# Four opening parts of the conditioning instead of two, six of their row blocks multiplied on TensorE in fp32

## What is computed

```
cond = jax.nn.silu(c) @ w_ada[l] + b_ada[l]
shift, scale, gate_raw = jnp.split(cond, 3, axis=-1)
h = x * (1.0 + scale[:, None]) + shift[:, None]
proj = h @ w_in[l]
```

## Time and profile before

| | us |
|---|---|
| median of 3 runs | 2113.29 (2106.57 to 2115.07) |
| profiled execution | 2106.91 |
| its span, first to last instruction | 2105.1 |
| PE busy in it | 1908.0 (91%) |
| DVE busy in it | 1003.5 (48%) |
| ACT busy in it | 855.7 (41%) |
| POOL busy in it | 695.8 (33%) |

### The profile page before, as it was taken

The page is one execution under the profiler, slowest core; times in us unless marked ns, Lnnn a source line. Parts: engine busy times, 40 slices in busy tenths (PEclk is TensorE's granted clock), DMA queues, the critical chain, the costliest instruction groups (busy, mean ns, idle before and its releaser), DMA issues.

```text
span 2105.1 us, 35718 instructions
## 1 busy us (share of the span) xinstructions
PE 1908.0 (91%) x14368; PEld 1523.4 (72%) x14368; DVE 1003.5 (48%) x1327; ACT 855.7 (41%) x1220; POOL 695.8 (33%) x486
## 2 busy tenths in 40 slices
PE   4999988899997999988799997989989999998977
PEld 3687877699774687877699774666756877776755
DVE  6566377633445118376632545668625213132232
ACT  2424465533523434465533524445534323333332
POOL 2454532300252335532300341333433543332312
PEclk9899999999998999999999999999999999999998
DMA  8662222200422322322200422312233221221211
GB/s 326 231 220 71 90 90 75 85 4 4 152 99 80 116 73 68 101 87 79 73 4 4 170 90 70 140 60 71 76 114 120 91 89 50 70 69 51 67 64 70
DMA packets 60827, 192.91 MB, mean 92 GB/s; under 512 B 5632, under 2 KB 5888, under 8 KB 60320
## 3 DMA queue, kind: packets, MB, share of 16 engines
q1 hardware_dynamic: 60704, 191.10, 26.4%
HBM read 173.25 MB, written 17.83 MB: 91 GB/s over the span
## 4 chain that ended last, share of the span: by engine, by line
issue 49%; PE 23%; POOL 18%; DVE 4%; ACT 4%; DMA 1%; POOLq 0%; DVEq 0%; ACTq 0%; SPq 0%
POOL w_lo_sb L716 17%; PE proj L1978 11%; PE aux L2187 3%; DVE area_sb L1288 2%; DMA w_raw_sb<-wall 1%; PE aux L2118 1%; PE aux L2244 1%; PE proj L2187 1%; PE aux L2241 1%; DVE area_sb L1552 1%; ACT L813 1%; ACT w_hi_sb L793 0%; DVE area_sb L1291 0%; ACT L921 0%; PE aux L2174 0%
## 5 line engine op out<-in xcount | busy, mean ns | idle before, releaser
L716 POOL TENSOR_TENSOR w_lo_sb<-w_raw_sb,w_hi_sb 128x512 fp32r<-128x512 f32 x462 | 677.6, 1487 | 1202.9 <-ACT w_hi_sb L793 1202.8
L1978 PE MATMUL proj<-act_hi_sb,w_hi_sb 128*128 128x512 f32 x1480 | 601.3, 406 | 28.3 <-POOL w_lo_sb L716 11.1
L1978 PE MATMUL proj<-act_hi_sb,w_lo_sb 128*128 128x512 f32 x1480 | 581.7, 393 | 0.0
L1978 PE MATMUL proj<-act_lo_sb,w_hi_sb 128*128 128x512 f32 x1480 | 581.6, 393 | 0.0
L793 ACT ACTIVATE w_hi_sb<-w_raw_sb 128x1024 fp32r<-128x1024 f32 x231 | 244.4, 1058 | 719.6 <-PE proj L1978 501.0
L1978 PEld LDWEIGHTS proj<-act_hi_sb,w_hi_sb 128*128 128x128 f32 x1480 | 281.6, 190 | 100.0 <-issue 33.0
L1978 PEld LDWEIGHTS proj<-act_lo_sb,w_hi_sb 128*128 128x128 f32 x1480 | 281.9, 190 | 62.0 <-issue 6.3
L1978 PEld LDWEIGHTS proj<-act_hi_sb,w_lo_sb 128*128 128x128 f32 x1480 | 281.1, 190 | 60.3
L1997 PE MATMUL aux<-act_hi_sb,w_hi_sb 128*128 128x512 f32 x336 | 138.0, 411 | 36.3 <-issue 23.4
L1288 DVE TENSOR_TENSOR area_sb<-area_sb 128x256 f32<-128x256 f32 (+2 forms) x208 | 140.6, 716 | 19.4 <-ACT area_sb L946 9.8
L1997 PE MATMUL aux<-act_lo_sb,w_hi_sb 128*128 128x512 f32 x336 | 135.2, 402 | 0.0
(11 more groups left out here) (251 smaller groups left out, 2558.7 us busy)
## 6 DMA issues: line engine op xcount, KB each, us to landing
w_raw_sb<-wall SPq DMA_DIRECT2D x231, 512.0 KB, 3.3
area_sb<-w_ada SPq DMA_DIRECT2D x32, 512.0 KB, 5.5
slots_sb<-w_ada SPq DMA_DIRECT2D x16, 512.0 KB, 8.3
gate_scr<-stage_sb SPq DMA_DIRECT2D x32, 256.0 KB, 2.2
area_sb<-gate_scr SPq DMA_DIRECT2D x8, 1024.0 KB, 9.1
x_scr<-area_sb SPq DMA_DIRECT2D x3, 2048.0 KB, 7.3
area_sb<-x_scr SPq DMA_DIRECT2D x3, 2048.0 KB, 10.2
area_sb<-lru_gates SPq DMA_DIRECT2D x1, 3584.0 KB, 13.1
```

The costliest lines, as they stand in the source:

```text
L716: nc.gpsimd.tensor_tensor(w_lo[:, b % 2, :, :].rearrange("p k n -> p (k n)")[:, half], w_raw[:, b % 2, half], w_hi[:, b % 2, :, :].rearran ...
L1978: ins = MM(bank, w[:, s, k, :], a[:, t, :], start=(start and i == 0), stop=(stop and i == len(terms) - 1))
```

## The change

Layer 0's conditioning comes in four parts q of 512 columns (shift and scale of channel tiles 2q and 2q+1) where it was two halves of 1024. w_ada's columns are rearranged for that outside the kernel. A load is 256 KB, and there are 32 of them, into twelve buffers in the same space. Part 0 has all eight row blocks on DVE; parts 1 to 3 have six (ADA_ROWS), and TensorE multiplies row blocks 6 and 7 from their load buffers by the column of c, in fp32, into the same PSUM column that takes the sum over DVE's accumulator. SP loads parts, x tiles and weight blocks 0 to 2 in turn. The derived columns follow all four parts on DVE.

```diff
+ADA_ROWS = (8, 6, 6, 6)
...
-            for half in range(2):
-                jobs.add(("ada", 0, half), 4 + half)
+            for q in range(4):
+                jobs.add(("ada", 0, q), 4 + q % 2)
...
-            def load_part(half, k):
-                n = KT * half + k
-                wait(sp, S("ada_used"), n - 5)
-                sp.dma_start(ada_part[:, n % 6], dram["w_ada"][0, k][:, D * half:D * half + D])\
-                    .then_inc(S(f"ada_part{n % 6}"), 16)
+            def load_part(q, k):
+                n = KT * q + k
+                if n > 11:
+                    old, row = (n - 12) // KT, (n - 12) % KT
+                    if row < ADA_ROWS[old]:
+                        sp.wait_ge(S("ada_used"), sum(ADA_ROWS[:old]) + row + 1)
+                    else:
+                        job_ready(sp, ("ada", 0, old))
+                sp.dma_start(ada_part[:, n % 12], dram["w_ada"][0, k][:, HALF * q:HALF * q + HALF])\
+                    .then_inc(S(f"ada_part{n % 12}"), 16)
...
-            for k in range(6):
-                load_part(0, k)
-            load_x(0)
-            load_x(1)
-            blocks_to(1)
-            load_part(0, 6)
-            load_part(0, 7)
-            load_x(2)
-            load_x(3)
-            blocks_to(2)
-            for k in range(KT):
-                load_part(1, k)
-            for m in range(4, KT):
-                load_x(m)
+            for q in range(4):
+                for k in range(KT):
+                    load_part(q, k)
+                load_x(2 * q)
+                load_x(2 * q + 1)
+                blocks_to(min(q + 1, 3))
...
-            conditioned(0, 0, ((0, 4), (8, 4)))
-            for m in range(5):
-                if m < 4:
+            for q in range(4):
+                for k in range(ADA_ROWS[q]):
+                    ada_part_step(q, k)
+                conditioned(0, q, ((2 * q, 2), (8 + 2 * q, 2)))
+                for m in (2 * q, 2 * q + 1):
                     modulated(0, m)
-                if m:
-                    low(SPLITS["h", 0] + m - 1, m - 1, ST[(m - 1) % 2])
-            for k in range(KT):
-                ada_part_step(1, k)
+                for m in (2 * q, 2 * q + 1):
+                    low(SPLITS["h", 0] + m, m, ST[m % 2])
...
-                def condition(half):
-
-                    pe.wait_ge(S("ada_used"), KT * (half + 1))
-                    x = job_open(pe, ("ada", 0, half))
-                    for j in range(8 * half, 8 * half + 8):
-
-                        at = 8 * (j % 8 // 4) + 4 * (j // 8) + j % 4
-                        ins = MM(x[:, at:at + 1], ada_acc[:, P * j:P * j + P], C("ones", 0, 1), start=True, stop=True)
-                    job_full(ins, ("ada", 0, half))
+                def condition(q):
+
+                    pe.wait_ge(S("ada_used"), sum(ADA_ROWS[:q + 1]))
+                    x = job_open(pe, ("ada", 0, q))
+                    rest = range(ADA_ROWS[q], KT)
+                    for k in rest:
+                        n = KT * q + k
+                        pe.wait_ge(S(f"ada_part{n % 12}"), 16 * (n // 12 + 1))
+                    for j in range(4):
+                        at = 8 * (j // 2) + 2 * q + j % 2
+                        ins = MM(x[:, at:at + 1], ada_acc[:, HALF * q + P * j:HALF * q + P * j + P], C("ones", 0, 1),
+                                 start=True, stop=not rest)
+                        for k in rest:
+                            ins = MM(x[:, at:at + 1], ada_part[:, (KT * q + k) % 12, P * j:P * j + P],
+                                     DV["c"][:, k:k + 1], start=False, stop=(k == KT - 1))
+                    job_full(ins, ("ada", 0, q))
...
-                             ready=lambda k: condition(1) if (l, k) == (0, 4) else None)
+                             ready=lambda k: condition(k // 2) if l == 0 and k in (2, 4, 6) else None)
```

More of the change, by code:

```diff
@@ L442, in build @@
         later_acc = area[:, 18:24].rearrange("p a t -> p (a t)")
[L443 removed]
+        ada_part = slots[:, 5:8].rearrange("p a b t -> p (a b) t")
         def wait(eng, semaphore, value):
@@ L1325, in ada_add, with ada_part_step @@
                 ins.then_inc(S("ada_used"), 1)
-            def ada_part_step(half, k):
-                n = KT * half + k
-                dve.wait_ge(S(f"ada_part{n % 6}"), 16 * (n // 6 + 1))
-                wait(dve, S("ada_used"), n)
-                ada_add(ada_acc[:, D * half:D * half + D], ada_part[:, n % 6], k)
+            def ada_part_step(q, k):
+                n, at = KT * q + k, sum(ADA_ROWS[:q]) + k
+                dve.wait_ge(S(f"ada_part{n % 12}"), 16 * (n // 12 + 1))
+                wait(dve, S("ada_used"), at)
+                ada_add(ada_acc[:, HALF * q:HALF * q + HALF], ada_part[:, n % 12], k)
             def later_step(n):
@@ L2554, in lay_out @@
     tiles = [gates[w, g, P * i:P * i + P, P * o:P * o + P] for g in range(4) for w in range(2) for o, i in BAND]
-    ada_cols = [D * s + HALF * half + np.arange(HALF) for half in range(2) for s in range(2)]
+    ada_cols = [D * s + 256 * q + np.arange(256) for q in range(4) for s in range(2)]
     w_ada = a["w_ada"][:, :, np.concatenate(ada_cols + [np.arange(2 * D, ADA)])].reshape(DEPTH, KT, P, ADA)
```

19 lines of the change are left out of this document (7 added, 12 removed).

## The result

| | before | after |
|---|---|---|
| median, runs on one chip (us) | 2106.97 (2102.27 to 2115.07, 9 runs) | 2119.16 (2114.57 to 2124.25, 9 runs) |
| profiled execution | 2106.91 | 2118.45 |
| its span | 2105.1 | 2116.7 |

What follows compares the result with a forecast made beforehand. The instant when ACT splits weight block 6 sets the pace: an early start of 3.6 us is eaten by three breaks of 5.5 us and the rows between, so 11 us later; 2113.3 + 11 = 2124 us, range 2111 to 2132.

Steps and rivals of the forecast that it cites:

- Start of the first part: Opening: ACT splits block 1 before the first high part, so TensorE starts at 24.5, not 28.09, a gain of 3.6 us.
- The cycle: Each of the four parts: dense matmuls, then condition, then tile making; 12.8 us each, part 3 starting at 63.4.
- (a): A part's 24 dense matmuls on TensorE: 7.8 us from the low clock, 5.45 from the full one; 7.3 taken.
- From the last tile to block 6: Low part, derived columns 3.04 us, later steps 7.99, issue and landing: ACT splits block 6 at 81.8 instead of 70.7.
- What a shift of block 6 is worth: Behind the opening: a shift of ACT's split of block 6 shifts the end as much, here 11 us.
- the prediction's own sign: Forecast wrong if the trace from 100 us on is not shifted by what block 6 was.
- A short queue at block 6: Rival at block 6's load: landing in 4.5 us, split at 79.0, +8.3 us, 2121.6; chance 0.20.
- Swallowed by the idle time behind: Rival behind block 6: TensorE's 3.9 us wait for ACT doesn't move along, +7 us, 2120; chance 0.13.
- No collisions: Rival in the parts: clock stays up, POOL's splits miss DVE's rows, part 3 at 57.6, +2 us, 2115; chance 0.10.
- Low clock in each condition: Rival in TensorE's conditions: each takes 5.3 us at the low clock, +20 us, 2133; chance 0.09.
- Fixed part in line: Rival in the loads: each load's fixed cost paid in line, at most +59 us for 16 more loads, 2172; chance 0.02.
- Faster: Rival for the whole kernel: the first part's 3.6 us reach the end, 2110 or less; chance 0.03.

## Why the prediction was right

The chain that was forecast is the one that the trace shows, and its sum to the split of block 6 is 0.7 us off, with terms that miss both ways. That the same 11 us stand at the end owes something to luck, as told below. The forecast of the median, 2124, was 4.8 us too high (2119.16), and not by the chain: it was added to 2113.3, the median of three runs, where nine runs of the same kernel have 2106.97. The ratio, 1.0066 for the 0.5% forecast, is free of that.

**Start of the first part: right.** ACT's second w_hi came at 21.12 (forecast 21.3) and TensorE's first dense matmul at 24.21 (24.5). The reason held too: with ACT's order changed, TensorE started at 18.45, and the 256 KB loads had nothing to do with it. Block 1 was split 0.2 us sooner than before, although eight more loads stood ahead of it, so no fixed part of 2 us was paid in line (it would have been 16 us). The smaller loads weren't free, though. From 6 to 20 us the queue carried 388 GB/s with them and 409 before; it is 378 to 390 in all nine profiled kernels with 256 KB loads and 405 to 409 in all five with 512 KB loads. Block 1 was split at 21.56 us on average in the nine and at 21.13 in the five: 0.4 us, of which the executions' different beginnings may be a part. The Trainium skill, "DMA: Bandwidth & Descriptors", section "Bandwidth", asks for DMAs of 1 MiB or more for at least 75% of peak. By that rule smaller loads are slower, and the traces agree in direction: 5% of the rate for half the size. The 2 us that the prediction took from the same page stand there for DMAs that GpSimd issues, and these are issued by SP.

**The cycle: right in its sum, with its terms off both ways.** Dense work up to the condition took 7.06, 7.65 and 7.96 us (forecast 7.8 for the first, 7.3 for the others). The condition took 2.73 (2.9) and the tile 2.59 (2.6). So the first cycle was 0.9 us shorter than forecast and the third 0.5 longer. The term that was mis-sized is (a): I took a middle between the two levels of the clock, and the clock fell in all three breaks. (The 1.45 us that POOL costs DVE's rows doesn't come out of its rows either: 4.39 less 2.7 is 1.7. It moved only the lower bound.) The starts of the parts, 36.59, 49.56 and 62.84, were each 0.6 to 1.2 us ahead of the forecast.

**From the last tile to block 6: right in its sum, one term wrong.** The derived columns took 5.1 us, not the 3.04 of the earlier trace rows. Five of their small operations, 128x4 each, took 3.02 us while POOL split block 4 (63.51 to 66.0), where one alone takes 0.16 or 0.17. Seen one by one, it is only two of them:

```profile
63.51 2.51 POOL L714 TENSOR_TENSOR w_lo_sb<-w_raw_sb,w_hi_sb 128x512 fp32r<-128x512 f32 x2 [6.79 <-ACT w_hi_sb L791]
63.61 1.19 DVE L1286 TENSOR_TENSOR derived_sb<-derived_sb 128x4 f32<-128x4 f32 x1
...
64.74 1.28 POOL L714 TENSOR_TENSOR w_lo_sb<-w_raw_sb,w_hi_sb 128x512 fp32r<-128x512 f32 x1
64.84 1.20 DVE L1286 TENSOR_TENSOR derived_sb<-derived_sb 128x4 f32<-128x4 f32 x1
```

Each started 0.1 us after one of POOL's two operations and ended with it (64.80 and 66.04, POOL's 64.79 and 66.02); the three behind them took 0.16 us each. I had priced POOL's splits into the row blocks and not into these. The later steps took 7.2 us, not 7.99, landing and ACT's start 6.6 us, not 6.4. Together with the earlier part 3 the split came at 82.50 instead of 81.8.

**What a shift of block 6 is worth: right at the near mark, not followed to the end.** The split moved by 11.8 us, M by 11.5, the end by 11.6. The near mark needs a condition that the prediction didn't name: block 6 sets the pace only where it comes late; once it is in time, the wait for block 9 is the next bound. Where block 6 was split 3.5 us earlier in the kernel before, M came 1.0 us later. And between M and the end the shift wasn't constant, as I had said that it would be; by the prediction's own sign (the trace from 100 us on shifted by what block 6 was) it was wrong there. Comparing the issue times of the same weight blocks, it was 11.7 us at 131, 4.6 to 4.8 from 578 to 905, and 11.2 from 1439 on. The mean granted clock of the stretches goes that way: before and after, 130 to 580 and 905 to 1440 us (columns as in the earlier trace rows):

```profile
130.00:580.00 450.00, 418.46 (x4967) 357.20 (x4967) 245.07 (x354) 209.42 (x320) 135.73 (x91) 0.97 0.25 83
...
905.00:1440.00 535.00, 484.73 (x5121) 390.09 (x5120) 301.21 (x432) 245.51 (x371) 148.17 (x106) 0.98 0.22 78
```

```profile
130.00:580.00 450.00, 420.69 (x5002) 359.34 (x5000) 249.99 (x358) 208.78 (x322) 142.33 (x93) 0.98 0.26 89
...
905.00:1440.00 535.00, 483.76 (x5112) 391.32 (x5111) 295.56 (x433) 243.19 (x369) 141.67 (x102) 0.96 0.22 76
```

One hundredth of 450 us is 4.5 us, and two of 535 are 10.7, both from rounded clocks: of the size of the 7.1 us by which the shift fell and the 6.4 by which it grew again. But a second profiled execution of the unchanged kernel was shorter than the first by 5 us at 389 and by 4.2 at the end:

> The kernel before once more, unchanged, for a second profile of it. In the first comparison the changed kernel's splits of weight blocks came 11.5 us later than before at 119 us, 4.6 us later from 580 to 900 us, and 11.3 us later from 1430 us to the end. Theory (the shift made in the opening is carried to the end, and the dip between is how the clock fell in the one profile of before): against this second profile the dip lies elsewhere or is gone, and the two profiles of the same kernel differ by several us somewhere between 200 and 1500 us. Rival (the opening's shift is given back and something later costs it again): the two profiles of before agree within 1 us all along, and the dip stays.

Its span was 2100.9 us, its time 2102.72. It was 0.7 us ahead of the first at 131 and 3.5 at 578. So some 3 us of the first stretch are the kernel's own spread between executions. Against this second profile the shift is 12.4 us at 131, 8.1 at 578, 8.7 at 905 and 15.4 from 1439 on: the dip is smaller and not gone. For the second stretch the two profiles of the kernel before agree within 0.3 us, and all but one of the other kernels lost 1 to 7 us against them there. Whether the change has a part in that clock, or it is where it happened to fall, stays open. That the two nearly cancel is luck for the forecast of 11 us: with the second profile it would have been 15.8. The timed runs, 9 against 9, give 12.2 us between the medians.

**The rivals.** A short queue at block 6: no, the landing took about 6.5 us, and the rival needed 4.5. Swallowed by the idle time behind: no, TensorE still waited 2.53 us there for ACT, where it had waited 3.92, so 1.4 us of it was swallowed, not 3.9. No collisions: no; the clock fell in every break. Low clock in each condition: not in the changed kernel, but measured in the kernel with the condition between the tiles. Fixed part in line: no, as told above. Faster: no; even with four of its faults taken away the scheme came level with the kernel before (1.0002). There ACT waits 9.30 us for block 9, as in the kernel before. That block 9 is what holds this version is read from its trace; the four parts with all weight blocks ahead, which would test it, weren't run, so whether a mended opening would gain behind that order stays open.

**The cause, in one line of the account.** Of the +11.5 us at M, 2.9 us go when the derived columns are moved, 3.8 when ACT makes the first tiles first, 8.3 with both, and 5.1 when SP issues block 6 without waiting for the later steps. Single shares needn't sum to a whole, because they are links of chains that meet at block 6, and whichever ends last decides. What is shown by one edit each is that these three, and the fp32 matmuls by 2.4 us of M, are links of it. That the half clock behind each break costs 2.4 us a part (12 matmuls by 0.427 instead of 0.228) is read from the rows and wasn't undone by an edit.

## What to carry to other kernels

Cutting an opening into more parts helps only if every engine's order has the first part first. Here ACT had a weight block ahead of it that only the second part needs. A result that stands behind dense work in the same engine's order comes as late as that work, however early its inputs are, and each further part pays that delay again. Before shaping the opening, look at what queue the next weight block waits in. One order of SP's issues made the kernel before 0.4% faster, where the four parts with all their mends only came level with it.

## What the runs showed of the hardware that I had not expected

- A DVE operation of 128x4, 0.16 us alone, took 1.19 us when it started just behind one of POOL's splits of 128x512: it ended 0.01 us after POOL's did. The same shows in the kernel with the derived columns early, where one small operation (128x2, 0.17 us alone) took from 15.01 to 16.26 beside a POOL operation from 14.97 to 16.24. So what counts is how many DVE operations start while POOL is at work, not their size. Two h of 128x512 took 2.86 us beside it and 1.00 alone.
- 256 KB loads carried 388 GB/s in a full queue, and 512 KB loads 409.
- Twelve fp32 matmuls of one column (24 records) behind dense work took 2.73 us at 2.4 GHz and 5.28 us at 1.2 GHz.
- Two executions of one kernel differed by 4.2 us in their spans, 0.7 of it by 131 us and 3.5 by 578, with a different share of low clock in between. For an effect of 10 us, a single profile tells which steps moved, not how much of the end they explain.
